# Two-block network on one core: block one's LayerNorms, its adaptive condition and the hand-over to the fills, rebuilt

## What is computed

```python
cond = silu(c)
mod = cond @ w_ada[l] + b_ada[l]
sh1, sc1, g1, sh2, sc2, g2 = split(mod, 6)
u = _layer_norm(h) * (1.0 + sc1) + sh1
z = u @ w_in[l]
...
h = _layer_norm(DEEPNORM_ALPHA * h + g1 * mix) * ln1_w[l] + ln1_b[l]
u2 = _layer_norm(h) * (1.0 + sc2) + sh2
a, bb = split(u2 @ w_ffn_in[l], 2)
ffn = (silu(a) * bb) @ w_ffn_out[l]
h = _layer_norm(DEEPNORM_ALPHA * h + g2 * ffn) * ln2_w[l] + ln2_b[l]
```

## Time and profile before

| | |
|---|---|
| median of 3 runs | 3309.01 us (3307.96 to 3311.09) |
| profiled execution, its own time | 3308.02 us |
| its span | 3305.9 us |
| mean granted TensorE clock | 0.971 |
| PE busy | 3128.1 us |
| POOL, DVE, ACT busy | 1440.2, 1153.4, 1085.3 us |

### The profile page before, as it was taken

How to read it: one execution, slowest core, us unless ns; L and a number is a source line. 1 busy time by engine, 2 the same in 40 slices (tenths; PEclk the granted TensorE clock), 3 DMA queues, 4 the chain that set the end, 5 groups by cost and what they waited for, 6 DMA issues and landing times.

```text
span 3305.9 us, 52329 instructions
## 1 busy us (share of the span) xinstructions
PE 3128.1 (95%) x20668; PEld 2496.1 (76%) x20668; DVE 1153.4 (35%) x1637; ACT 1085.3 (33%) x1516; POOL 1440.2 (44%) x1824
## 2 busy tenths in 40 slices
PE   6998989988999899999988999999999999899999
PEld 4887768857887586887666888788688866688877
DVE  5016442332111355322555422225632255442210
ACT  2445453323222324112444322222411244432222
POOL 3542234634555363322415655566322241555555
PEclk7999889989999899999999999999999999999999
DMA  4223332212333232222414232233221241423233
GB/s 192 95 89 118 112 119 85 95 55 70 101 95 98 72 117 73 88 66 102 152 55 156 91 97 95 96 108 122 73 87 63 100 159 55 153 89 101 95 96 121
DMA packets 101407, 330.85 MB, mean 100 GB/s; under 512 B 9856, under 2 KB 10112, under 8 KB 100224
## 3 DMA queue, kind: packets, MB, share of 16 engines
q1 hardware_dynamic: 74656, 273.85, 25.3%
q10 hardware_dynamic: 26592, 54.66, 4.5%
HBM read 299.64 MB, written 28.84 MB: 99 GB/s over the span
## 4 chain that ended last, share of the span: by engine, by line
issue 41%; POOL 30%; PE 24%; DMA 1%; DVE 1%; ACT 1%; DVEq 0%; POOLq 0%; SPq 0%; ACTq 0%
POOL w_lo L310 30%; PE psum L339 19%; PE psum L620 4%; DMA w_raw<-in_fills 1%; DMA H<-scratch 1%; DVEq L1409 0%; PE psum L796 0%; POOLq L306 0%; PE psum L816 0%; PE psum L834 0%; POOLq L316 0%; DVE HL L1412 0%; PE psum L836 0%; DVE arena L1966 0%; PE psum L830 0%
## 5 line engine op out<-in xcount | busy, mean ns | idle before, releaser
L310 POOL TENSOR_TENSOR w_lo<-w_raw,w_hi 128x256 fp32r<-128x256 f32 x1820 | 1440.0, 822 | 1860.8 <-ACT w_hi L870 1664.9
L339 PE MATMUL psum<-XH,w_hi 128*128 128x512 f32 x2592 | 1061.8, 410 | 35.7 <-DVE XL L1412 22.5
L339 PE MATMUL psum<-XH,w_lo 128*128 128x512 f32 x2592 | 1021.2, 394 | 0.0
L339 PE MATMUL psum<-XL,w_hi 128*128 128x512 f32 x2592 | 1019.8, 393 | 0.0
L870 ACT ACTIVATE w_hi<-w_raw 128x1024 fp32r<-128x1024 f32 x436 | 460.2, 1056 | 813.6 <-PE psum L339 717.7
L339 PEld LDWEIGHTS psum<-XH,w_hi 128*128 128x128 f32 x2592 | 493.5, 190 | 174.0 <-issue 59.2
L339 PEld LDWEIGHTS psum<-XL,w_hi 128*128 128x128 f32 x2592 | 492.6, 190 | 106.3
L339 PEld LDWEIGHTS psum<-XH,w_lo 128*128 128x128 f32 x2592 | 493.7, 190 | 103.7 <-issue 9.4
L339 PE MATMUL psum<-HH,w_hi 128*128 128x512 f32 x976 | 391.6, 401 | 29.5 <-DVE HL L1412 21.5
L339 PE MATMUL psum<-HL,w_hi 128*128 128x512 f32 x976 | 387.0, 397 | 0.0
L339 PE MATMUL psum<-HH,w_lo 128*128 128x512 f32 x976 | 386.7, 396 | 0.0
(11 more groups left out here) (302 smaller groups left out, 2385.6 us busy)
## 6 DMA issues: line engine op xcount, KB each, us to landing
w_raw<-in_fills SPq DMA_DIRECT2D x488, 512.0 KB, 3.6
scratch<-arena ACTq DMA_DIRECT2D x86, 256.0 KB, 2.0
arena<-scratch ACTq DMA_DIRECT2D x10, 1024.0 KB, 8.7
arena<-in_w_ada SPq DMA_DIRECT2D x4, 2048.0 KB, 20.1
H<-scratch ACTq DMA_DIRECT2D x4, 2048.0 KB, 15.7
scratch<-H SPq DMA_DIRECT2D x2, 2048.0 KB, 8.5
arena<-scratch ACTq DMA_DIRECT2D x2, 2048.0 KB, 9.9
arena<-scratch ACTq DMA_DIRECT2D x2, 1792.0 KB, 20.8
```

Of the source, the lines that this page charges most:

```text
L310: ins = nc.gpsimd.tensor_tensor(w_lo[:, to:to + FILL // 4], w_raw[:, of:of + FILL // 4], w_hi[:, to:to + FILL // 4].bitcast(F32), ALU.subt ...
L339: ins = mm(out_ap, wt[:, w:w + 128], xt[:, x0:x0 + T], start=first and k == 0 and o == 0, stop=last and k == n - 1 and o == 2)
```

## The change

**Loads.** SP loads only the two matrices that are needed at once (identity, ones) and a few tail columns of the constants, then `par1`, x in four quarters with a semaphore each, the first two fills, and then the four parts of `w_ada` with a semaphore each. ACT issues the rest of the constants and `par2` after its first hand-over and waits for them ahead of its first take.

**Condition.** `weighted_rows` and the single-column matmuls against `w_ada` are gone. Each part of `w_ada` is multiplied as a whole: eight matmuls with 32 stationary columns in four column groups over 512 columns (`condition_rows`), an ACT copy (`rows_out`), four single-column matmuls (`condition_columns`). Three rounds run before the first fill, the fourth between pieces of fills 0 and 1 (`half_fill`). Parts 2 and 3 carry the scales of channel tiles 0 to 3 and 4 to 7.

**LayerNorms 2 and 3.** LayerNorm 3's mean is worked out from the statistics of LayerNorm 2: `residual` also keeps a sum weighted by `ln1_w` (`WSUM`), which one matmul sums over channels. DVE forms Q, which is the centred value times `ln1_w` less a mean, while PE sums the squares; multiplied by the first reciprocal deviation it is the second LayerNorm's centred input but for the bias, and ACT squares it with that bias. `H` is written after the hand-over. DVE's running sum leaves the last tile to a second matmul over `H`.

**Hand-over.** DVE, ACT and DVE again pass single tiles (`ln_u`, `ln_hi`, `ln_x`), and `first_two` multiplies two fills by each tile as it comes, here and in all calls of `gemm_rms`, where the matmul of the sum of squares now follows both. For LayerNorm 3 and LayerNorm 4 ACT applies scale and shift.

The diff, cut to its core and moved left by eight columns. Left out: renamed helpers, shifted semaphore counts, the removed bodies of `layer_norm`, `norm_hi`, `norm_lo` and `residual`.

```diff
-    sp.dma_start(con[:], dram["con"]).then_inc(sem("const_in"), 16)
+    tail = CONST["cd"]
+    sp.dma_start(con[:, 0:256], dram["con"][:, 0:256]).then_inc(sem("const_in"), 16)
+    sp.dma_start(con[:, tail:], dram["con"][:, tail:]).then_inc(sem("const_in"), 16)
     sp.dma_start(par1[:], dram["par1"]).then_inc(sem("const_in"), 16)
-    sp.dma_start(par2[:], dram["par2"]).then_inc(sem("const_in"), 16)
-    sp.dma_start(H[:], dram["x"]).then_inc(sem("x_in"), 16)
-    for k in range(4):
-        sp.dma_start(A(40 + 16 * k, 16 * KB), dram["w_ada"][k]).then_inc(sem(f"ada_in{min(k, 1)}"), 16)
+    for q in range(4):
+        part = slice(2 * q * T, (2 * q + 2) * T)
+        sp.dma_start(H[:, part], dram["x"][:, part]).then_inc(x_in[q], 16)
     for f in range(2):
         sp.dma_start(w_raw[:, f * FILL:(f + 1) * FILL], dram["fills"][f]).then_inc(w_loaded[f], 16)
+    for k in range(4):
+        sp.dma_start(A(40 + 16 * k, 16 * KB), dram["w_ada"][k]).then_inc(sem(f"ada_in{k}"), 16)
...
+    def first_two(f, c, skew, ready, tiles=range(DT)):
+        for k in tiles:
+            if k == 0:
+                for j in range(2):
+                    pe.wait_ge(chunk_out[j], c + skew * SKEW[j])
+            ready(k)
+            for j in range(2):
+                if k == 0:
+                    pe.wait_ge(lo_ready, f + j + 1)
+                ins = blocks(j, XH, XL, bank(j), [k], [k], k == 0, k == DT - 1)
+                if k == DT - 1:
+                    ins.then_inc(fill_done, 1)
+    def next_two(f, c, skew):
+        for j in range(2, 4):
+            pe.wait_ge(lo_ready, f + j + 1)
+            if c:
+                pe.wait_ge(chunk_out[j], c + skew * SKEW[j])
+            blocks(j, XH, XL, bank(j), range(DT), range(DT), True, True).then_inc(fill_done, 1)
     def gemm_rms(f, c, n, x, norm, skew):
-        for j in range(4):
-            pe.wait_ge(lo_ready, f + j + 1)
-            pe.wait_ge(chunk_out[j], c + skew * SKEW[j])
-            blocks(j, XH, XL, bank(j), range(8), range(8), True, True,
-                   None if j else lambda k: pe.wait_ge(sem("rms_x"), x + k + 1)).then_inc(fill_done, 1)
-            if j == 0:
-                sum_of_squares(norm)
+        first_two(f, c, skew, lambda k: pe.wait_ge(sem("rms_x"), x + k + 1))
+        sum_of_squares(norm)
+        next_two(f, c, skew)
         gemm(f + 4, c + 1, n, skew=skew)
...
+    def residual_sum(acc):
+        pe.wait_ge(sem("acc"), acc)
+        mm(bank(4), C("ones", 128), A(ACC_KB), start=True, stop=False)
+        pe.wait_ge(sem("acc"), acc + 1)
+        mm(bank(4), C("ones", 128), H[:, (DT - 1) * T:], start=False, stop=True).then_inc(sem("ln_sum"), 1)
+    def squares_sum(n):
...
+    pe.wait_ge(sem("const_in"), 48)
+    mm(bank(7, 16), C("ones", 128), P1("ln1_w", 0, 16), start=True, stop=True).then_inc(sem("ada_used"), 1)
+    for t in range(DT):
+        if t % 2 == 0:
+            pe.wait_ge(x_in[t // 2], 16)
+        ins = mm(bank(4), C("ones", 128), H[:, t * T:(t + 1) * T], start=t == 0, stop=t == DT - 1)
+    ins.then_inc(sem("ln_sum"), 1)
+    squares_sum(0)
+    def condition_rows(k):
+        pe.wait_ge(sem(f"ada_in{k}"), 16)
+        w = A(40 + 16 * k, 16 * KB).rearrange("p (t k c) -> p t k c", k=DT, c=128)
         for kt in range(DT):
-            mm(bank(6, 1, t), A(40, 128, (t * DT + kt) * 128), cond[:, kt:kt + 1], start=kt == 0, stop=kt == DT - 1)
+            g = 32 * (kt % 4)
+            ins = mm(bank(6 + k % 2)[g:g + 32], A(COND_KB, 32, 32 * kt), w[:, :, kt, :], start=kt < 4, stop=kt >= 4)
+        ins.then_inc(sem("ada_done"), 1)
+    def condition_columns(k):
+        pe.wait_ge(sem("ada_row"), k + 1)
+        for t in range(4):
+            ins = mm(bank(k, 1, t), A(ROW_KB, 128, k % 2 * T + 128 * t), C("ones", 1), start=True, stop=True)
+        ins.then_inc(sem("ada_used"), 1)
     pe.wait_ge(sem("cond"), 2)
-    for t in range(4, ADA_FIRST):
-        ins = mm(bank(6, 1, t), A(40, 128, t * DT * 128), C("ones", 1), start=True, stop=True)
-    ins.then_inc(sem("ada_used"), 1)
-
-    gemm(0, 0, 32, ready=by_pairs("ln_x", 0))
+    for k in range(3):
+        condition_rows(k)
+        condition_columns(k)
+    normed_1 = lambda t: pe.wait_ge(sem("ln_x"), t + 1)
+    def half_fill(j, tiles):
+        for t in tiles:
+            normed_1(t)
+            blocks(j, XH, XL, bank(j), [t], [t], t == 0, False)
+    pe.wait_ge(lo_ready, 1)
+    half_fill(0, range(4))
+    condition_rows(3)
+    pe.wait_ge(lo_ready, 2)
+    half_fill(1, range(2))
+    condition_columns(3)
+    half_fill(1, range(2, 4))
+    first_two(0, 0, 0, normed_1, range(4, DT))
+    next_two(0, 0, 0)
+    gemm(4, 1, 28)
...
+    residual_sum(1)
+    pe.wait_ge(sem("acc"), 3)
+    mm(bank(6), C("ones", 128), A(WSUM_KB), start=True, stop=True).then_inc(sem("ln_sum"), 1)
+    squares_sum(2)
+    squares_sum(3)
+    first_two(88, 22, 0, lambda k: pe.wait_ge(sem("ln_x"), DT + k + 1))
+    next_two(88, 22, 0)
+    gemm(92, 23, 40)
     gemm2816(132, 33, FT)
-    layer_norm(4, None, lambda t: A(16, T, t * T), acc=4)
+    residual_sum(4)
+    squares_sum(4)
...
+    def squares(n):
         for q in range(4):
             act.wait_ge(sem("ln_xc"), 4 * n + q + 1)
-            fn(sq(2 * q), xc(2 * q), ACT.Square).then_inc(sem("ln_sq"), 1)
...
+            fn(A(16, 2 * T, 2 * q * T), A(0, 2 * T, 2 * q * T), ACT.Square).then_inc(sem("ln_sq"), 1)
+    def ln_rstd(n, kb):
+        act.wait_ge(sem("ln_var"), n + 1)
+        rstd("ln", 5, 1.0 / D, 0, A(kb), "ln_rstd")
...
+    ln_exp_tables()
+    squares(0)
+    for f in range(2):
         first_hi(f)
-    norm_hi(0, "ln")
+    ln_rstd(0, RSTD_KB)
...
+    def rows_out(k):
+        act.wait_ge(sem("ada_done"), k + 1)
+        fn(A(ROW_KB, T, k % 2 * T), bank(6 + k % 2), ACT.Copy).then_inc(sem("ada_row"), 1)
+    def first_x(t):
+        act.wait_ge(sem("ln_u"), t + 1)
+        fn(XH[:, t * T:(t + 1) * T], A(16, T, t * T), ACT.Copy).then_inc(sem("ln_hi"), 1)
+    for k in range(3):
+        rows_out(k)
+    for t in range(4):
+        first_x(t)
+    rows_out(3)
+    first_hi(2)
+    for t in range(4, DT):
+        first_x(t)
+    first_hi(3)
+    tail = CONST["cd"]
+    act.dma_start(con[:, 256:tail], dram["con"][:, 256:tail]).then_inc(sem("const_in"), 16)
+    act.dma_start(par2[:], dram["par2"]).then_inc(sem("const_in"), 16)
...
+    act.wait_ge(sem("const_in"), 80)
...
+    ln_exp_tables()
     gemm(80, 80, 8)
-    layer_norm(2, two(0), two(16))
-    layer_norm(3, two(0), two(16))
-    norm_hi(1, "ln")
+    squares(2)
+    ln_rstd(2, RSTD_KB)
+    for t in range(DT):
+        act.wait_ge(sem("ln_xc"), 12 + t // 2 + 1)
+        ins = fn(A(16, T, t * T), A(Q_KB, T, t * T), ACT.Square, bias=lbt[:, 16 + t:17 + t])
+        if t % 2:
+            ins.then_inc(sem("ln_sq"), 1)
+    ln_rstd(3, RSTD2_KB)
+    for t in range(DT):
+        act.wait_ge(sem("ln_u"), DT + t + 1)
+        for to in (A(16, T, t * T), XH[:, t * T:(t + 1) * T]):
+            ins = fn(to, A(0, T, t * T), ACT.Identity, scale=mod[:, 32 + t:33 + t], bias=mod[:, 24 + t:25 + t])
+        ins.then_inc(sem("ln_hi"), 1)
...
+    ln_exp_tables()
...
+    squares(4)
+    ln_rstd(4, RSTD_KB)
+    for q in range(4):
+        act.wait_ge(sem("ln_u"), 2 * DT + q + 1)
+        for t in (2 * q, 2 * q + 1):
+            fn(H[:, t * T:(t + 1) * T], A(0, T, t * T), ACT.Identity, scale=P1("ln2_w", t), bias=P1("ln2_b", t))
+        nc.scalar.drain()
+        for t in (2 * q, 2 * q + 1):
+            rms_hi(0, "norm1", t)
...
+    def centred(n, mean):
...
+        dve.wait_ge(sem("ln_sum"), mean)
...
+            stt(chunks(A(0, 2 * T, 2 * q * T), T), bc(bank(4), 2), -1.0 / D, chunks(Ht(2 * q, 2), T), ALU.mult, ALU.add)\
+                .then_inc(sem("ln_xc"), 1)
+    def low(n, t):
+        dve.wait_ge(sem("ln_hi"), n + t + 1)
+        s = slice(t * T, (t + 1) * T)
+        lo(XL[:, s], A(16, T, t * T), XH[:, s]).then_inc(sem("ln_x"), 1)
...
+    def residual(f, step, gate, weighted=False):
+        for t in range(DT):
+            h = Ht(t, 1)
+            dve.wait_ge(fill_done, f + step * (t + 1))
+            ins = stt(h, bank(t % 4), mod[:, gate + t:gate + t + 1], h, ALU.mult, ALU.add)
+            ins.then_inc(chunk_out[t % 4], 1)
+            drain()
+            if 0 < t < DT - 1:
+                ins = tt(A(ACC_KB), A(ACC_KB) if t > 1 else Ht(0, 1), h, ALU.add)
+                if t == DT - 2:
+                    ins.then_inc(sem("acc"), 1)
+            if t == DT - 1:
+                cp(small[:, 48:49], small[:, 48:49]).then_inc(sem("acc"), 1)
+            if weighted:
+                w = lbt[:, 8 + t:9 + t]
+                if t == 0:
+                    ins = ts(A(WSUM_KB), h, w, None, ALU.mult)
+                else:
+                    ins = stt(A(WSUM_KB), h, w, A(WSUM_KB), ALU.mult, ALU.add)
+                if t == DT - 1:
+                    ins.then_inc(sem("acc"), 1)
...
+    dve.wait_ge(sem("cond"), 1)
+    drain()
```

(78 more changed lines are left out.)

103 lines of the change are left out of this document (15 added, 88 removed).

## The result

The changed kernel takes 3253.33 us (median of 4 runs, 3249.02 to 3257.21) beside 3308.49 for the kernel before on the same chip (4 runs, 3307.26 to 3311.09): ratio 0.9832, 95% interval 0.9815 to 0.9849. The profiled execution took 3252.76 (span 3251.0), 55.3 less than the one before; its mean granted clock is 0.981, before 0.971.

A forecast was written before the change was run, and what follows sets the result against it. PE, busy 95% of the span, was taken as the bound, leaving only its idle time to win. Start 12.7, middle 22.3 and last LayerNorm 4.7 sum to 39.7; 3308.0 less that is 3268.3, as median 3269 (range 3259 to 3280).

The forecast's parts named there:

- Zero, up to 2 lost at each of three: Block two's RMS norms: two fills sharing each tile gain nothing, at most 2 us lost at each of three norms.
- the rest of the trace shifted, PE's waits of block two unchanged: Expected sign in the trace: outside the changed places everything only moves in time, and block two's PE waits stay.
- Start: From x's loading through the condition to fill 3: fill 3 ends at 73.5 for 86.2, gain 12.7 us (7 to 19).
- three rounds: Condition rounds before the first fill: 4.7 us each, 14.1 in all, ending at 38.3.
- the clock charge of 1.8: Condition rounds at the start: 1.8 us added for two rounds partly at 1.2 GHz (0 to 6).
- Middle: Block one, last projection fill to next fill: first fill matmul at 730.4 against 752.74, gain 22.3 us (18 to 24).
- Last LayerNorm: End of block one: fill at 1139.2 against 1143.89, gain 4.7 us (3 to 6).
- the wait on the constants: ACT ahead of fill 0's take: fill 4's parts ready near 70 against 73.5; costs only if landing takes past 9 us.
- rival D: ACT's take of fill 0 or fill 93 waits on constants or late H, 6 to 10 us: 3277; chance 0.12.
- A: Condition rounds: column groups don't overlap with 512 columns, 7.1 for 2.1 a round, 20 us in all: 3289; chance 0.07.
- B: Block one: clock stays up, fills begin at 2.4 GHz, 7 us more gained: 3262; chance 0.17 for this or better.
- C: Shared fill pairs: hand-over starves PE into 1.2 GHz, 9.6 us a pair, 57 at six: 3326; chance 0.02.

The follow-up runs named there:

- experiment 1: Changed kernel measured again unaltered: 3258.0 us; and changed kernel with the old fill order at block two's three inner RMS norms: 3252.11 us.
- rms_old: Changed kernel with one fill alone, then the sum of squares, again at the three RMS norms inside block two: 3252.11 us, ratio 0.9831.
- serial_groups: Changed kernel with all eight matmuls of each condition round in one column group, one after the other: 3277.87 us, ratio 0.99.
- shift_after: Changed kernel with two extra unread matmuls of constants (1.7 us) ahead of one round of fills in block two's first layer: 3255.65 us.
- warm: Changed kernel with unread matmuls of constants filling PE's idle gaps at the start, middle and last LayerNorm: 3253.09 us, ratio 0.9828.
- no_split: Changed kernel with all four condition rounds ahead of the fills, fills 0 and 1 then sharing all eight tiles: 3249.75 us, ratio 0.9823.

## Why the prediction was wrong

**The failed step** is the one on block two: "Zero, up to 2 lost at each of three", with "the rest of the trace shifted, PE's waits of block two unchanged". For the edit of `gemm_rms` itself it holds (experiment 1). For the stage it does not: 9.3 us came there. Of the 15.6 by which the sum missed (55.3 − 39.7), 6.2 are mis-sized terms (4.5, 0.8 and 0.9, below), 9.3 block two, 0.1 what the other stages add up to; without block two the time would lie inside the range. What the runs show in its place: PE does block two's work with 15.3 us less of busy time, since less of it falls at 1.2 GHz (low clock 77.1 before, 47.2 after), and waits 6.0 longer. The new code of block two is not the reason: rms_old has the old order there and takes 2121.4, serial_groups has the changed kernel's program there and takes 2129.3 with 64.8 of low clock. I had treated the clock as a property of each place; with the same program in block two it differs from kernel to kernel. Low clock alone does not give the length: with 60.7 to 64.8 of it four kernels took, less the work put in, 2121.2 to 2129.3, and the seven with 47.1 to 53.7 all took 2121.4 to 2122.3. All three profiles of before have 2130 to 2131. That all this is due to where block one's change puts block two in time is argued, since shift_after did not give the rise that it asked for. Why the kernel before falls so regularly on the long side stays open.

**Start, 12.7 forecast, 17.2 measured: mis-sized.** The first fill was forecast at 43.0 and came at 39.09; from there to fill 3's take it is 30.0 (forecast 30.5). Of the 3.9, three rounds gave 3.2 (3.62 each for 4.7), the clock charge of 1.8 was not due (windows above, 1.00) and the hand-over gave 0.3; against them the sums over x ended 1.4 later than forecast (first sum matmul 6.96 for 5.4, sums' end 16.07 for 14.7), which hid part of the error. In the round the term that was off is the single columns: 1.8 from L440's 0.22 each, which ran at 0.50 granted; at the full clock they are 1.05/8 = 0.13. The column groups took 1.92 where I took 2.1 between 1.8 and 2.8. Inside its bounds (7 to 19), the term alone moves the forecast to 3264.5.

**Middle, 22.3 forecast, 23.1 measured (53.54 − 30.47): right.** 31 us of gap became 30.5. The second sum took the forecast time (9.26). The first was shorter (7.13 for 9.32, behind a wait of 1.55 instead of 2.41), and so no longer covers Q to its end: Q is done at 696.9 (L1828, 691.46 + 5.39), 0.6 after the reciprocal deviation. ACT's two writes a tile take 1.43 where I took 1.25. The late write of `H` is there as described (DVE is free for the next product at 732.50, fill 88 was taken at 725.69) and hidden, since the gain holds up to high part 97.

**Last LayerNorm, 4.7 forecast, 5.6 measured (25.84 − 20.20): right**, and so was the wait on the constants: ACT waits 3.43 for them, until 58.81, but PE shows no wait from 52.30 to 78, so rival D did not come.

**Rivals.** A is refuted by the 1.92. Of B only the 1.8 of the rounds came; the half fill still ran at 1.2 GHz (window 40 to 44, 0.50), and warm shows that 1.8 more are in the middle. C: the shared pairs did not starve into 1.2 GHz; fills 88 and 89 took 12.1 (713.57 to 725.7) for the 13 forecast, and the window 714 to 728 has 0.88 granted. The range was wrong since it allowed nothing for the 2130 us of block two, 64% of the span.

## What to carry to other kernels

A long stage that a change does not touch can still move by 0.3% of the total through TensorE's clock: read several profiles of the kernel before, compare stages by a mark that counts work (here the high parts), and widen the range by what that stage does. Kernels with about the same low clock there (60.7 to 64.8) lay 8 us apart, so read PE's busy and idle time beside it. Price small matmuls from rows at the clock that the new place will have. Splitting a small job to start the main one earlier pays only if the first pieces can be fed: here the main work started 3.4 later and ended 2.8 earlier.

## What the runs showed of the hardware

- Matmuls with 32 stationary columns over 512 float32 positions: 16 instructions take 7.05 in one column group and 1.92 in four groups side by side.
- Single-column float32 matmuls: 0.22 an instruction at a granted 0.50, 1.05/8 = 0.13 at 1.00.
- Rounds with ACT between them (waits of 0.72 us) kept the full clock from 24 to 36 us. Then it fell: in the changed kernel around PE's wait of 2.61 ahead of the first fill (0.78, then 0.50), and in no_split just as well, where PE waited only 0.72 and 0.28 (0.83, then 0.75). In the kernel before it fell while PE had no wait at all: 64 single-column instructions ran from 30.10 for 11.08 us, and from 36 to 40 PE is busy 4.00 at a granted 0.50. So the length of the last wait does not decide it.
- In block two the same 15114 PE instructions took 2061.2 us of busy time before and 2045.9 after, with 72.7 and 43.4 us of it at 1.2 GHz.
- Within one program the mean granted clock and the time go together, roughly: runs of before with 0.976 took 3296.5, with 0.973 3304.2 and 3304.8, with 0.969 3306.2 to 3313.0, with 0.967 and 0.966 3314.7 and 3315.1.
- An ACT activation with scale and bias read per partition starts every 0.71 us (714.01, 714.73), a write of 0.80; two of them a tile set the pace of a hand-over.
